# Norms by halves of the tokens between 512-token products, and four weight slots with the lower weights over the raw ones

## What is computed

```python
# first block, last layer (attention), latent tokens only
x = x + mod_x[2] * y_x
x = x + mod_x[5] * sqrelu_mlp(rms_norm(x, norm2_g[layer]) * (1 + mod_x[4]) + mod_x[3], mlp_w1[layer], mlp_w2[layer])
...
# second block, both layers: layer norms of ALPHA * x + gate * f(x)
y = (xf - mu) * lax.rsqrt(var + LN_EPS)
return (y * g.astype(jnp.float32) + b.astype(jnp.float32)).astype(x.dtype)
```

## Time and profile before

| | us |
|---|---|
| median of 3 runs | 2777.05 (2775.76 to 2779.73) |
| the profiled execution | 2776.3 |
| its span, first to last instruction | 2774.6 |
| TensorE busy | 2634.4 (95%) |
| VectorE busy | 1599.4 (58%) |
| ScalarE busy | 938.9 (34%) |

### The profile page before, as it was taken

One profiled execution on the slowest core, in us unless ns is written; L12 is line 12 of the kernel. 1 busy time (PEld: TensorE's weight loads), 2 busy tenths in 40 slices (PEclk: granted clock), 3 DMA queues, 4 the chain that ended last, 5 costly groups with the idle time before them and its releaser, 6 DMA issues.

```text
span 2774.6 us, 34838 instructions
## 1 busy us (share of the span) xinstructions
PE 2634.4 (95%) x13096; PEld 2139.5 (77%) x13096; DVE 1599.4 (58%) x2349; ACT 938.9 (34%) x1322; POOL 96.1 (3%) x185
## 2 busy tenths in 40 slices
PE   7999998999999988998999999989999898899997
PEld 7888787888888866666788877767777677688885
DVE  4877636554556555664655565665556765544445
ACT  2324423121212243763332234253322353523233
POOL 0000000000000000000000000000000000000000
PEclk9999998999999989999999999989999899899998
DMA  6332322333333311001455553224545332122222
GB/s 253 129 129 92 107 76 69 108 112 109 110 107 127 106 55 60 1 1 61 143 162 164 166 187 105 84 86 149 159 151 188 123 103 84 58 94 91 98 92 68
DMA packets 81461, 303.11 MB, mean 109 GB/s; under 512 B 9041, under 2 KB 9169, under 8 KB 80337
## 3 DMA queue, kind: packets, MB, share of 16 engines
q1 hardware_dynamic: 55296, 206.82, 22.4%
q0 software_dynamic: 26064, 94.91, 10.6%
HBM read 299.60 MB, written 2.10 MB: 109 GB/s over the span
## 4 chain that ended last, share of the span: by engine, by line
PE 86%; DVE 7%; ACT 5%; issue 1%; DMA 0%; DVEq 0%; SPq 0%; ACTq 0%
PE G L413 21%; PE G L415 21%; PE G L414 21%; PE G L440 5%; PE G L441 5%; PE G L442 5%; PE B L513 1%; ACT Whi L864 1%; PE B L764 1%; PE G L724 1%; PE B L475 1%; PE B L740 1%; DVE Wlo L1286 1%; ACT hs_hi L1189 1%; PE B L467 1%
## 5 line engine op out<-in xcount | busy, mean ns | idle before, releaser
L1286 DVE TENSOR_TENSOR Wlo<-Wraw,Whi 128x1024 fp32r<-128x1024 f32 x357 | 437.2, 1225 | 874.3 <-ACT Whi L864 873.7
L864 ACT ACTIVATE Whi<-Wraw 128x1024 fp32r<-128x1024 f32 x357 | 378.0, 1059 | 1167.2 <-PE G L415 931.6
L413 PE MATMUL G<-h_hi,Whi 128*128 128x512 f32 (+1 forms) x1040 | 371.7, 357 | 3.1 <-DVE Wlo L1286 3.1
L415 PE MATMUL G<-h_hi,Wlo 128*128 128x512 f32 (+1 forms) x1040 | 366.1, 352 | 0.0
L414 PE MATMUL G<-h_lo,Whi 128*128 128x512 f32 (+1 forms) x1040 | 365.8, 352 | 0.0
L415 PE MATMUL G<-hid_hi,Wlo 128*128 128x512 f32 (+1 forms) x840 | 309.8, 369 | 0.0
L413 PE MATMUL G<-hid_hi,Whi 128*128 128x512 f32 (+1 forms) x840 | 309.7, 369 | 0.0
L414 PE MATMUL G<-hid_lo,Whi 128*128 128x512 f32 (+1 forms) x840 | 309.5, 368 | 0.0
L413 PE MATMUL G<-hs_hi,Whi 128*128 128x512 f32 x768 | 306.4, 399 | 1.9 <-DVE SQ L2006 1.9
L415 PE MATMUL G<-hs_hi,Wlo 128*128 128x512 f32 x768 | 303.3, 395 | 0.0
L414 PE MATMUL G<-hs_lo,Whi 128*128 128x512 f32 x768 | 303.3, 395 | 0.0
(11 more groups left out here) (342 smaller groups left out, 4026.0 us busy)
## 6 DMA issues: line engine op xcount, KB each, us to landing
Wraw<-wstream_dram SPq DMA_DIRECT2D x357, 512.0 KB, 3.3
Araw<-adaw_dram POOLq DMA_DIRECT2D x180, 512.0 KB, 3.7
FIRST<-firstw_dram SPq DMA_DIRECT2D x4, 1536.0 KB, 22.2
X<-xin_dram SPq DMA_DIRECT2D x4, 1536.0 KB, 11.3
out_dram<-X SPq DMA_DIRECT2D x8, 256.0 KB, 2.0
ROW<-rows_dram SPq DMA_DIRECT2D x2, 768.0 KB, 6.2
CB<-cvec_dram SPq DMA_DIRECT2D x2, 512.0 KB, 5.4
CB<-cvec_dram POOLq DMA_DIRECT2D x1, 512.0 KB, 5.0
```

The costliest lines, as they stand in the source:

```text
L413: pe.matmul(o, wh, hi[:, a:b], start=(k == 0), stop=False)
L415: last = pe.matmul(o, wl, hi[:, a:b], start=False, stop=(k == kt - 1))
L864: act.activation(Whi[:, t % 2, :], Wraw[:, t % 4, :], ACT.Copy).then_inc(w_hi, 1)
L1286: dve.tensor_tensor(Wlo[:, t % 2, :], Wraw[:, t % 4, :], Whi[:, t % 2, :].bitcast(F32), ALU.subtract).then_inc(w_lo, 1)
```

## The change

**Weights.** `Whi` and `Wlo` get four slots each. `Wlo` lies on the memory of `Wraw`: the lower weight is written over the raw one. So a load now waits for the product of the unit four before, and the split of unit t waits for its own load and for product t-4. The places that had the wait for a product only through the split now wait for it by themselves (`evac`, behind the split).

```diff
-        Wraw = sb("Wraw", [P, 4, D])
-        Whi = sb("Whi", [P, 2, D], F32R)
-        Wlo = sb("Wlo", [P, 2, D], F32R)
+        ws = ExitStack()
+        Wraw = sb("Wraw", [P, 4, D], where=ws)
+        ws.close()
+        Wlo = sb("Wlo", [P, 4, D], F32R)
+        Whi = sb("Whi", [P, 4, D], F32R)
...
             def load(t):
-                wait(sp, w_lo, t + -3)
+                wait(sp, tile_done, t + -3)
...
-                wait(act, tile_done, t + -1)
-                act.activation(Whi[:, t % 2, :], Wraw[:, t % 4, :], ACT.Copy).then_inc(w_hi, 1)
+                wait(act, tile_done, t + -3)
+                act.activation(Whi[:, t % 4, :], Wraw[:, t % 4, :], ACT.Copy).then_inc(w_hi, 1)
 
             def evac(t):
 
                 split_hi(t + 2)
+                wait(act, tile_done, t + 1)
```

```diff
+            def edge_end(e, t0, src, kt):
+
+                for p in range(2):
+                    for j in range(4):
+                        t = At(t0 + j)
+                        if p == 0:
+                            wait(pe, w_lo, t + 1)
+                            if j < 2:
+                                wait(pe, tile_free[t % 2], t // 2)
+                            else:
+                                pe.wait_ge(e_a_used, 4 * e + j - 1)
+                        elif j >= 2:
+                            wait(pe, tile_free[t % 2], t // 2)
+                        for k in range(kt):
+                            last = part_product(t, src, p, k, kt, k == 0, k == kt - 1)
+                        last.then_inc((e_a_done, tile_done)[p], 1)
+                        if p == 1 and j == 0:
+                            edge_stats(e, 0)
+                        if p == 1 and j == 1:
+                            edge_spread(e, 0)
+
+            def edge_start(e, t0, src, sset):
+
+                for p in range(2):
+                    for k in range(KD):
+                        for u in range(2):
...
+                            last = part_product(t, src, p, k, KD, k == 0, k == KD - 1)
+                            if p == 1 and k == KD - 1:
+                                last.then_inc(tile_done, 1)
+                        if p == 0 and k == 1:
+                            edge_stats(e, 1)
+                        if p == 0 and k == 4:
+                            edge_spread(e, 1)
```

`part_product` is the three matmuls of one k-tile on 256 columns. VectorE's part of an edge, from the fourth of the eight products on (`residual(j, p)` adds half p of product t0+j, `add` sums, `moments` makes variance and reciprocals, `shift` is the LayerNorm's pair or the RMS norm's one operation, `lower` the lower activation; each on 256 columns):

```diff
+                split_lo(At(t0 + 2))
+                residual(0, 0)
+                add(None, 3)
+                split_lo(At(t0 + 3))
+                residual(1, 0)
+                add(0, 4)
+                middle(5)
+                residual(2, 0)
+                add(0, 5)
+                residual(3, 0)
+                add(0, 6)
+                add(0, 7)
+                residual(0, 1)
+                add(1, 4)
+                moments(0)
+                residual(1, 1)
+                add(1, 5)
+                if more:
+                    split_lo(At(t0 + 4))
+                dve.wait_ge(e_spread, 2 * e + 1)
+                shift(0, 0)
+                shift(0, 1)
+                lower(0, 0)
+                if more:
+                    split_lo(At(t0 + 5))
+                residual(2, 1)
+                add(1, 6)
+                shift(0, 2)
+                lower(0, 1)
+                shift(0, 3)
+                lower(0, 2)
+                residual(3, 1)
+                add(1, 7)
+                for k in range(4, KD):
+                    shift(0, k)
+                    lower(0, k - 1)
+                lower(0, KD - 1)
+                moments(1)
+                dve.wait_ge(e_spread, 2 * e + 2)
```

More of the change, by code:

```diff
@@ L481, in norm_stats, with part_product @@
                 last.then_inc(spread_done, 1)
+            def part_product(t, src, p, k, kt, first, last):
+                hi, lo = src(k)
+                a, b = NC + 256 * p, NC + 256 * (p + 1)
+                wh, wl = Whi[:, t % 4, k * P:(k + 1) * P], Wlo[:, t % 4, k * P:(k + 1) * P]
+                o = G[t % 2][:, a:b]
+                pe.matmul(o, wh, hi[:, a:b], start=first, stop=False)
+                pe.matmul(o, wh, lo[:, a:b], start=False, stop=False)
+                return pe.matmul(o, wl, hi[:, a:b], start=False, stop=last)
@@ new lines, in edge_stats @@
+            def edge_stats(e, p):
+                bank = (B4, B6)[p]
+                pe.wait_ge(e_acc, 11 * e + (7, 11)[p])
+                for b in range(2):
+                    last = pe.matmul(bank[:, b:b + 1], RS[:, 256 * p + b * P:256 * p + (b + 1) * P], ones[:, 0:1],
+                                     start=True, stop=True)
+                if e > 0:
+                    for b in range(2):
+                        last = pe.matmul(bank[:, 4 + b:5 + b], Junk[:, 256 * p + b * P:256 * p + (b + 1) * P],
+                                         ones[:, 0:1], start=True, stop=True)
+                last.then_inc(e_col, 1)
@@ new lines, in edge_spread @@
+            def edge_spread(e, p):
+                bank = (B4, B6)[p]
+                pe.wait_ge(e_rstd, 2 * e + p + 1)
+                for b in range(2):
+                    last = pe.matmul(bank[:, 512 + b * P:512 + (b + 1) * P],
+                                     RCOL[:, 12 * p + b:12 * p + b + 1].to_broadcast([P, P]), ident, start=True, stop=True)
+                if e > 0:
+                    for b in range(2):
+                        last = pe.matmul(bank[:, 768 + b * P:768 + (b + 1) * P],
+                                         RCOL[:, 12 * p + 2 + b:12 * p + 3 + b].to_broadcast([P, P]), ident, start=True,
+                                         stop=True)
+                last.then_inc(e_spread, 1)
@@ L920, in mlp @@
-                t0, h0_ = t0 + 16 * n, h0_ + CH * n
-                chunk(None)
-                freed(act, At(t0 + 2 * CH - 1))
-                after(KD - 1)
+                if edge is not None:
+                    chunk(None, 0)
+                    with act.Fori(0, n - 1) as i:
+                        chunk(i, 1)
+                else:
+                    with act.Fori(0, n) as i:
+                        chunk(i, 0)
+                chunk(None, n, last=True)
+                freed(act, At(t0 + 16 * (n + 1) - 1))
@@ L1212, in _ @@
                     evac(At(t0 + t))
-                    g = ps(G[(t0 + t) % 2], NC, NT)
+                    g = half(G[(t0 + t) % 2]) if l == 1 and t < 2 else ps(G[(t0 + t) % 2], NC, NT)
                     free = tile_free[(t0 + t) % 2]
@@ L2007, in chunk @@
                                           ALU.mult).then_inc(tile_free[(t + 1) % 2], 1)
[L2008 removed]
+                        dve.wait_ge(ffhi, fn + 1)
                         dve.tensor_tensor(hid2[1][:, j, :], SQ[:, j % 2, 0:NX], hid2[0][:, j, :].bitcast(F32),
                                           ALU.subtract).then_inc(hid_ready, 1)
[L2011 to L2013 removed]
+                    t2 = t1 + 24 * c0 + 2 * n_up
@@ L2041, in pack @@
+                edge(2 + 2 * l, t2 + 4, lambda m: MOD[:, l, 0, 40 + m:41 + m], down_middle, ln_shift(2 + 2 * l),
+                     ln_lower(2) if l == 0 else lambda p, k: None, more=(l == 0))
 def pack(x):
```

519 lines of the change are left out of this document (329 added, 190 removed).

## The result

| | before | after |
|---|---|---|
| median, us | 2778.07 (4 runs) | 2727.41 (2723.94 to 2730.09, 4 runs) |
| span of the profiled execution | 2774.6 | 2727.1 |
| mean granted clock | 0.972 | 0.981 |

The ratio is 0.9818 (95% interval 0.9801 to 0.9835). 2727.4 lies inside the range (2723 to 2763), 13.6 us under the forecast of 2741, outside the forecast's own range (2730 to 2750) and next to the first rival's 2729. 47.5 us of span went, where 36.1 were forecast. Was the rival's reason the right one, or did the sum leave something out? The experiments are about that.

The account below looks back on a forecast made before the run. TensorE, 95% busy, was taken as the bound, so only its waits and low clock could yield. Gains 26.8 + 4.4 + 2.9 + 1 + 2 - 1 = 36.1 off 2776.3 gave 2740.2, forecast 2741; range 2723 to 2763, own 2730 to 2750.

Parts of the forecast that it names:

- the first rival: TensorE's clock stays up where products wait on norms, and all waits outside them go: 2729 us, chance 0.17.
- The edges: Five norm places, 0 (RMS norm before last MLP) to 4 (last LayerNorm): gains 4.7, 7.2, 4.5, 7.2, 4.8 us; 26.8 after cuts.
- the low clock: TensorE at clock 0.50 during edge 1: only stats, spread and catching up count, 1.1 us; at edge 0, 1.4.
- Everywhere else TensorE had no wait that could go: Outside the rebuilt norms, only unchanged norms (4.4), hybrid mixer's end (2.9), SQ (1) and Wlo (2) yield time.
- the pair of splits: Upper and lower weight made before a norm's residual; moved away, the residual starts 2.2 us earlier at two unchanged norms.
- the halves: Products and norm at the five edges in token halves of 256 columns, A's norm running beside B's products.
- The tables: Spatial gate's tables, loaded after edge 2's norm; VectorE waits for them before its next weight split: costs 1 us.
- The overlap: Rival: it fails at the edges, A's norm starting only when B is done; no change, 2775 us, chance 0.03.
- ScalarE's 256-wide step: In the rival on VectorE's order making new waits, 0.70 us like 512-wide: 4.3 more at three edges, 2767, chance 0.05.
- late weights: Rival: loads wait for product t-4's end and, landing in 15 us, delay some 240 products: 2861 us, chance 0.05.
- The clock that stays low through each start: Rival: TensorE's clock stays low through each edge, pieces of 1.4 us bind instead of 1.09: 2754 us, chance 0.20.
- the wait for the sums under 10: Sign of being right: TensorE's wait before the sums of the norms falls from 36.3 us to under 10.

Follow-up runs that it names:

- the slots alone: The kernel before with four slots for upper and lower weights, the lower over the raw ones, norms not rebuilt in token halves: 2742.65 us, ratio 0.9872.
- the old wait with four slots: Four weight slots on the kernel before, but ScalarE's split of unit t still waits for product t-2: 2778.5 us, ratio 1.0000.

## Why the prediction was right in its range and low in its gain

- **The edges** held. Forecast costs 10.5, 19.3, 22.0, 19.3 and 21.5, together 92.6; measured (same way of counting) 9.9, 18.7, 22.3, 18.4 and 22.1, together 91.4. The third feed-forward product starts 28.2 us behind the mixer's last matmul (27.6 forecast), with 0.84 for Wlo (1).
- Inside that, terms were off and offset each other by luck. The step of VectorE was 1.09 in the sum; it is 1.12 and 1.24 by turns, 1.18 on average, since every second lower activation waits for ScalarE. The 1.1 for the low clock was 0.2 or less in this profile at edges 1 to 3 (0.9 in others), and edge 0's 1.4 some 0.7. The 0.04 for each cut, 1.6 in all, does not exist: 256-column matmuls start 0.117 apart, half of 0.2335.
- **The step that failed** is "Everywhere else TensorE had no wait that could go". It left 10.3 us outside the edges; measured are some 20 (34.7 with the slots alone, of which the edges themselves are 13.0, and 0.9 in the first stage are no effect). Norms 1 and 2 gave 2.9 and 2.6 (2.2 each), the hybrid end's wait 2.7 (2.9), the wait for Wlo 1.0 (2), SQ and the first feed-forward 2.8 and more (1), the attention 2.3 and the mixers 1.6 each (nothing). These rows stood in the list of waits of before, and each is a result that VectorE or ScalarE reached late. I had asked of each wait whether a weight stood in it, when the question was whether a split stood ahead of its producer.
- For the same reason the credit was given wrongly. In the forecast the pair of splits was worth 2.2 at each of four edges and 10.3 outside, 19 in all, and the halves some 17. The slots brought 34.7 (33.8 without what the first stage does by itself), the halves on top of them 12.8 (14.9 without the first stage).
- **The tables** were named, at 1 us; they and the clock behind them took 2.2, all that the halves gave at edge 2.
- **Rivals.** The overlap came about; ScalarE's 256-wide step is 0.50 and not 0.70; late weights were refuted by the old wait with four slots and by the landing of 3.7. The clock that stays low through each start was not there: 0.66 to 0.83 granted at edge 1 where that rival had 0.50. The clock that stays up was not there either.
- Of the signs, the wait for the sums under 10 did not come as written (16.2 in all; 9.9 at the edges alone). Waits in the middle of a stage that had none did appear, 1.4 and 0.5 behind edge 2, and were a good sign: they are where that edge's gain went. ScalarE waiting for Wraw was a bad one: it now waits 467 us for it, in the time in which it waited for TensorE before.

The rows' 0.13 us for each extra instruction of VectorE came from two different operations. One operation at both widths, in the changed kernel, gives 2 x 0.420 - 0.685 = 0.155 for each cut:

```profile
L1612 DVE TENSOR_TENSOR RS<-RS,SQ 128x256 f32<-128x256 f32 x40 | 16.8, 420 | 2.1 <-ACT SQ L1051 2.1
...
L1612 DVE TENSOR_TENSOR RS<-RS,SQ 128x512 f32<-128x512 f32 x15 | 10.3, 685 | 0.0
```

But durations overlap, and a chain runs by its steps from start to start: 0.33 to 0.34 at 256 wide and 0.59 to 0.61 at 512 (the sums of before, from 1803.03 and 1804.41), 0.07 or so for each cut. The sum had taken steps of 0.33, so the 0.13 entered only a rival, and the edges cost 91.4 together where the sum had 92.6. The clock stood at a granted 0.50 at half B's sums of edges 1 to 3 (from 1791.0, 2183.4 and 2325.5, two us each), behind waits of 2.01, 1.36 and 2.03. There it lay beside VectorE's chain and was free but for the edges where it reached the spread.

## What to carry to other kernels

When a buffer's depth is doubled, look at every instruction that stands in an engine's queue behind the one that waited for the buffer, and at who waits for those: here 34.7 us came from such places, more than the rebuilt norms added. And when an engine's clock is low somewhere, ask for each of its results whether the next engine is already waiting for it: at half B's sums it was not, at the spread it was. Before a second engine's work is reordered, see how far the other engine of the same loop is from binding; VectorE's 1.18 us and ScalarE's two operations of 0.50 were less than 0.2 apart, so a third operation cost its full price and a shorter VectorE gave little. And a stage that is made shorter brings forward what it had covered: the tables and the low clock behind edge 2 took back all that the halves gave there.

## What I had not expected of the hardware

- 24 matmuls of 256 columns took 2.80 us, 0.117 each: half of the 0.2335 of one of 512 columns.
- With filler matmuls in the gaps of edge 1 the granted clock was 1.00 in all three stretches, where it was 0.83, 0.66 and 0.76 without, and the edge was as long but for 0.2 us.
- The same spread of half B took 1.2 us in 20 of 30 LayerNorm edges and 2.1 in 8; edges built alike differed within one profile.
- At edge 1 of the changed kernel a 256-wide operation of VectorE that needed the result of the one before started 0.45 us behind it, an independent one 0.33 to 0.34.
